# Down projections of a decoder layer: eight of 22 contraction slices as a block product with seven products instead of eight, per pair of output tiles

## The reference, cut to what matters

```python
D_MODEL, D_FF = 1024, 2816

def swiglu(x, w_gu, w_down):
    g, u = jnp.split(x @ w_gu, 2, axis=-1)
    return (jax.nn.silu(g) * u) @ w_down

def trunk_layer(x, ...):
    f1 = swiglu(rmsnorm(x, norm_ffn1_pre), w_ffn1_gu, w_ffn1_down)
    x = x + 0.5 * rmsnorm(f1, norm_ffn1_post)
    mix, state = mixer(rmsnorm(x, norm_mix_pre), ...)
    x = x + rmsnorm(mix, norm_mix_post)
    f2 = swiglu(rmsnorm(x, norm_ffn2_pre), w_ffn2_gu, w_ffn2_down)
    return x + 0.5 * rmsnorm(f2, norm_ffn2_post), state
```

## Time and profile before

| | |
|---|---|
| three runs | 1361.54, 1366.59, 1367.52 us; median 1366.59 |
| the profiled execution | 1366.81 us, its span 1364.8 us |
| PE busy | 1329.4 us (97%) |
| DVE, ACT busy | 874.6 (64%), 566.9 us (42%) |
| mean granted clock of TensorE | 0.986 of 2.4 GHz |
| first down stage | 253.5 to 385.9 us |
| last down stage | 1218.2 to 1350.6 us |

### The profile page before, as it was taken

One profiled execution on the slowest core, in us unless ns is written; L12 is line 12 of the kernel. 1 busy time (PEld: TensorE's weight loads), 2 busy tenths in 40 slices (PEclk: granted clock), 3 DMA queues, 4 the chain that ended last, 5 costly groups with the idle time before them and its releaser, 6 DMA issues. The chain is left out here.

```text
span 1364.8 us, 30387 instructions
## 1 busy us (share of the span) xinstructions
PE 1329.4 (97%) x11729; PEld 1247.5 (91%) x11729; DVE 874.6 (64%) x1689; ACT 566.9 (42%) x1064; POOL 145.1 (11%) x275
## 2 busy tenths in 40 slices
PE   8999999999999999999999999999899999999996
PEld 8999999999989978888789888869899999999995
DVE  5998899822277544554553566664899999983225
ACT  5455555722254334444352332233554555463221
POOL 0000000000003105555551000000000000000000
PEclk9999999999999999999999999979999999999998
DMA  4232233322245627777776133314252223332221
GB/s 161 92 124 93 94 105 125 129 86 85 93 158 189 214 85 218 240 212 219 204 224 246 48 124 142 125 48 157 80 189 94 93 96 119 123 112 98 87 83 66
DMA packets 81075, 180.20 MB, mean 132 GB/s; under 512 B 12137, under 2 KB 46954, under 8 KB 79146
## 3 DMA queue, kind: packets, MB, share of 16 engines
q1 hardware_dynamic: 72746, 161.56, 34.6%
q0 software_dynamic: 8192, 16.79, 4.3%
HBM read 162.01 MB, written 16.30 MB: 131 GB/s over the span
## 5 line engine op out<-in xcount | busy, mean ns | idle before, releaser
L921 PE MATMUL acc<-x_forms,pair_w 128*128 128x272 f32 x1728 | 273.1, 288 | 0.0
L921 PEld LDWEIGHTS acc<-x_forms,pair_w 128*128 128x128 f32 x1728 | 244.2, 188 | 0.0
L2029 DVE TENSOR_TENSOR w_lo<-w_raw,w_hi 128x1024 fp32r<-128x1024 f32 (+1 forms) x92 | 125.4, 1363 | 126.5 <-ACT w_hi L1435 126.5
L998 PE MATMUL acc<-x_hi,w_hi 128*128 128x272 f32 x656 | 199.5, 304 | 0.0
L998 PE MATMUL acc<-x_hi,w_lo 128*128 128x272 f32 x656 | 191.8, 292 | 0.0
L998 PE MATMUL acc<-x_lo,w_hi 128*128 128x272 f32 x656 | 191.6, 292 | 0.0
L1435 ACT ACTIVATE w_hi<-w_raw 128x1024 fp32r<-128x1024 f32 (+1 forms) x92 | 107.5, 1169 | 143.6 <-PE acc L740 79.7
L450 POOL DMA_DIRECT2D pg<-in_lat x256 | 138.3, 540 | 200.1 <-issue 134.7
L998 PEld LDWEIGHTS acc<-x_hi,w_hi 128*128 128x128 f32 x656 | 123.6, 188 | 9.5 <-issue 7.9
L998 PEld LDWEIGHTS acc<-x_lo,w_hi 128*128 128x128 f32 x656 | 123.7, 188 | 5.2 <-issue 4.7
L740 PE MATMUL acc<-h_hi,w_hi 128*128 128x272 f32 x616 | 127.2, 288 | 0.0
(11 more groups left out here) (394 smaller groups left out, 2535.4 us busy)
## 6 DMA issues: line engine op xcount, KB each, us to landing
w_pair<-in_w_gu SPq DMA_DIRECT2D x68, 512.0 KB, 4.2
pg<-in_key_t SPq DMA_DIRECT2D x256, 96.0 KB, 2.5
w_raw<-in_w_dn SPq DMA_DIRECT2D x32, 704.0 KB, 4.1
w_raw<-in_w_in SPq DMA_DIRECT2D x44, 512.0 KB, 4.4
pg<-in_lat POOLq DMA_DIRECT2D x256, 64.0 KB, 2.8
w_raw<-in_w_gu SPq DMA_DIRECT2D x20, 512.0 KB, 3.8
x_mid<-x SPq DMA_DIRECT2D x2, 2176.0 KB, 7.1
g_mid<-sq SPq DMA_DIRECT2D x16, 272.0 KB, 3.4
```

What stands on the lines that cost most here:

```text
L921: ins = nc.tensor.matmul(bank, w[:, k * P:(k + 1) * P], v[:, k, :], start=start and k == 0 and term == 0, stop=k == KD // 2 - 1 and term == 2,
L998: ins = nc.tensor.matmul(acc[0][:, a, 0:HT], w[:, i % 2, k * P:(k + 1) * P], v[:, k, a * HT:(a + 1) * HT], start=k == 0 and term == 0, sto ...
L2029: nc.vector.tensor_tensor(wlo[:, slot, 0:tiles * P], raw[:, slot, 0:tiles * P], f32(whi[:, slot, 0:tiles * P]), ALU.subtract).then_inc(w_s ...
```

## The change

KC = 14 slices of h stay direct: units have seven slices (896 columns), 42 matmuls. The other eight slices (7 to 10 and 18 to 21) form a 2 x 2 x 2 block product for each pair of output tiles: two tiles, two groups of four slices, two token halves. Seven products of four slices, three terms and one half (12 matmuls each) take the place of eight. For that ACT and DVE make, once per stage, four differences of h blocks and seven high and low parts of them (`form`, `form_hi`, `form_lo`, 4 x 272 = 1088 columns each), and once per pair four sums of weight blocks (`block_sums`) and seven splits (`block_hi_part`, `block_lo_part`, 512 columns each). The weight blocks lie in the ends of the unit slots and in freed buffers, so SP loads those of a pair when PE has used those of the pair before. The results are put together by two copies on ACT and seven additions on DVE (`take`, 272 columns). The last two tiles, not one, are summed by halves; the second half of tile 7's direct units comes last. x is loaded again in two parts.

The core of the diff, without the bookkeeping of counters, semaphores and the helpers that only name buffers:

```diff
 STAGE = {}
 _u = _g = 0
-for _name, _n, _t, _gr in (("gu1", NC, KD, NC), ("dn1", 2 * KD, 11, KD), ("in", 44, KD, 0),
-                           ("out", KD, KD, KD), ("gu2", NC, KD, NC), ("dn2", 2 * KD, 11, KD)):
+for _name, _n, _t, _gr in (("gu1", NC, KD, NC), ("dn1", 2 * KD, KC // 2, 1), ("in", 44, KD, 0),
+                           ("out", KD, KD, KD), ("gu2", NC, KD, NC), ("dn2", 2 * KD, KC // 2, 1)):
...
+        HALF_C = KC // 2
+        DIRECT = list(range(HALF_C)) + list(range(KF // 2, KF // 2 + HALF_C))
...
+        NORMAL, LAST = [A11, S1, S2, A12, S4, S3, A22], [A11, S1, S2, S4, S3, A22, A12]
+        HI_FIRST = [A11, A12, A22, S1, S2, S4, S3]
+        TAKE_NORMAL = ["part", "y11", "y12", "pg", "tq", "y22", "y21"]
+        TAKE_LAST = ["part", "y12", "pg", "y22", "tq", "y21", "y11"]
...
+            def down_stage(name, q):
+                for p in range(4):
+                    weight_units(name, 4 * p, 2)
+                    if p:
+                        sp.wait_ge(dn_used, 7 * (4 * q + p))
+                    else:
+                        sp.wait_ge(pair_split, 7 * (NP * (q + 1) - 1))
+                    for i, n in enumerate((A11, A12, S4, A22)):
+                        sp.dma_start(block_raw[n][:], weights[name][4 * p + i][:, HALF_C * P:]).then_inc(dn_raw, 16)
+                    if p == 0:
+                        sp.wait_ge(pair_used, 7 * NP * (q + 1))
+                        sp.dma_start(x[:, 0:KD // 2, :], (x_mid if q else xT)[:, 0:KD // 2, :]).then_inc(x_again, 16)
+                    weight_units(name, 4 * p + 2, 2)
+                sp.wait_ge(dn_used, used_of(q, 3, S2))
+                sp.dma_start(x[:, KD // 2:KD, :], (x_mid if q else xT)[:, KD // 2:KD, :]).then_inc(x_again2, 16)
...
-            def down(name, h_at):
-                u0, n, _, g0, _ = STAGE[name]
-                def body(i):
-                    for j in range(4):
-                        start = isinstance(i, int) and i == 0 and j < 2
-                        if isinstance(i, int) and i == n // 4 - 1 and j >= 2:
-                            if j == 2:
-                                U, G = 4 * i + u0 + 2, 2 * i + g0 + 1
-                                last_by_half("f1post" if name == "dn1" else "f2post",
-                                             [(U, G, 1, range(11), True, False), (U + 1, G, 1, range(11, KF), False, True)],
-                                             hhi, hlo)
-                            continue
-                        unit(4 * i + (u0 + j), j % 2, 2 * i + (g0 + j // 2), j // 2, hhi, hlo,
-                             range(11 * (j % 2), 11 * (j % 2) + 11), j % 2 == 0, j % 2 == 1,
-                             h_ready if start else None, h_at + 11 * (j % 2))
-                trips(pe, n // 4, body)
...
+                def direct(u, sides, start):
+                    pe.wait_ge(w_split, u0 + u + 1)
+                    for n in range(KC // 2):
+                        k = DIRECT[HALF_C * (u % 2) + n]
+                        if u < 2:
+                            pe.wait_ge(h_ready, KC * q + HALF_C * u + n + 1)
+                        for term, (w, v) in enumerate(((whi, hhi), (whi, hlo), (wlo, hhi))):
+                            for a in sides:
+                                ins = nc.tensor.matmul(acc[u // 2 % 2][:, a, 0:HT], w[:, u % 2, n * P:(n + 1) * P],
+                                                       v[:, k, HALF[a]], start=start and n == 0 and term == 0,
+                                                       stop=u % 2 == 1 and n == KC // 2 - 1 and term == 2,
+                                                       skip_group_check=True)
+                        if sides == (1,) and u % 2 == 0 and n == 3:
+                            sum_half(norm, 0)
+                    return ins
+                def product(p, n):
+                    pe.wait_ge(dn_split, split_of(q, p, n))
+                    if p == 0:
+                        pe.wait_ge(hf_split, 7 * q + NORMAL.index(n) + 1)
+                    if n == A11:
+                        if p:
+                            pe.wait_ge(dn_kept, 2 * (4 * q + p))
+                        else:
+                            pe.wait_ge(gate_done, 2 * NP * (q + 1))
+                            pe.wait_ge(part_taken, 5 * NP * (q + 1))
+                    elif n == S2:
+                        pe.wait_ge(dn_kept, 2 * (4 * q + p) + 1)
+                    elif p and n in (S1, S3):
+                        pe.wait_ge(dn_taken, taken_of(q, p - 1, "part" if n == S1 else "tq"))
+                    start = n in (A11, S1, S3) or (p == 3 and n == A22)
+                    v_hi, v_lo, _ = h_form(n)
+                    for k in range(KD // 2):
+                        for term, (w, v) in enumerate(((block_hi[n], v_hi), (block_hi[n], v_lo), (block_lo[n], v_hi))):
+                            ins = nc.tensor.matmul(bank_of[n], w[:, k * P:(k + 1) * P], v[:, k, :],
+                                                   start=start and k == 0 and term == 0,
+                                                   stop=k == KD // 2 - 1 and term == 2, skip_group_check=True)
+                    ins.then_inc(dn_used, 1)
+                for p in range(4):
+                    last = p == 3
+                    if p:
+                        pe.wait_ge(dn_taken, taken_of(q, p - 1, "y12"))
+                    for i in range(2):
+                        direct(4 * p + i, (0, 1), i == 0).then_inc(w_used, 1)
+                    if p:
+                        pe.wait_ge(dn_taken, taken_of(q, p - 1, "y21"))
+                    for i in range(2):
+                        ins = direct(4 * p + 2 + i, (0,) if last else (0, 1), i == 0)
+                        if not last:
+                            ins.then_inc(w_used, 1)
+                    for n in (LAST if last else NORMAL):
+                        product(p, n)
+                pe.wait_ge(dn_taken, taken_of(q, 3, "y21"))
+                direct(14, (1,), False).then_inc(w_used, 1)
+                pe.wait_ge(dn_taken, taken_of(q, 3, "y11"))
+                direct(15, (1,), False).then_inc(w_used, 1)
...
-                        hi_part(u0 + NC, 0, 11)
-                        for k in range(6):
+                        hi_part(u0 + NC, 0, KC // 2)
+                        for k in range(8):
                             split_h_hi(q, k)
                     silu(s, 0)
...
                 nc.scalar.preload_act_table_set(LOG_EXP)
-                for k in range(6, 11):
+                for k in range(8, 11):
                     split_h_hi(q, k)
-                hi_part(u0 + NC + 1, 1, 11)
-                for k in range(11, KF):
+                hi_part(u0 + NC + 1, 1, KC // 2)
+                for k in range(11, KC):
                     split_h_hi(q, k)
...
+                act.wait_ge(pair_used, 7 * NP * (q + 1))
+                form_hi(A11)
+                form_hi(S1)
+                unit_hi(2)
+                form_hi(S2)
+                form_hi(A12)
+                block_hi_part(0, A11)
+                unit_hi(3)
+                block_hi_part(0, A12)
+                block_hi_part(0, A22)
+                form_hi(S4)
+                block_hi_part(0, S1)
+                block_hi_part(0, S2)
+                form_hi(S3)
+                form_hi(A22)
+                block_hi_part(0, S4)
+                block_hi_part(0, S3)
+                for p in range(4):
+                    if p < 3:
+                        unit_hi(4 * p + 4)
+                    act.wait_ge(dn_used, used_of(q, p, A11))
+                    if p:
+                        act.wait_ge(dn_taken, taken_of(q, p - 1, "y21"))
+                    nc.scalar.activation(rpre[:, HALF[0]], acc[2][:, 0, 0:HT], ACT.Copy).then_inc(dn_kept, 1)
+                    if p < 3:
+                        unit_hi(4 * p + 5)
+                    act.wait_ge(dn_used, used_of(q, p, S2))
+                    nc.scalar.activation(rpre[:, HALF[1]], acc[2][:, 0, 0:HT], ACT.Copy).then_inc(dn_kept, 1)
+                    if p < 3:
+                        act.wait_ge(dn_taken, taken_of(q, p, "y12"))
+                        square(norm, 2 * p)
+                        act.wait_ge(dn_taken, taken_of(q, p, "y21"))
+                        square(norm, 2 * p + 1)
+                        unit_hi(4 * p + 6)
+                        for n in HI_FIRST[:5]:
+                            block_hi_part(p + 1, n)
+                        unit_hi(4 * p + 7)
+                        for n in HI_FIRST[5:]:
+                            block_hi_part(p + 1, n)
+                act.wait_ge(dn_taken, taken_of(q, 3, "y12"))
+                square_half(norm, KD - 2, 0)
+                act.wait_ge(dn_taken, taken_of(q, 3, "y22"))
...
+                def form(i):
+                    out, a, b = ((t1, b12, b11), (t3, b22, b12), (t2, b22, t1), (t4, b21, t2))[i]
+                    if i == 0:
+                        dve.wait_ge(h_full, KF * (q + 1))
```

(57 more changed lines are left out.)

177 lines of the change are left out of this document (130 added, 47 removed).

## The result

| | before | after |
|---|---|---|
| median of the runs | 1365.6 us (5 runs, 1361.54 to 1367.52) | 1379.44 us (5 runs, 1376.49 to 1379.8) |
| ratio | | 1.0101, interval 1.008 to 1.0122 |
| profiled execution, its span | 1366.81, 1364.8 us | 1376.49, 1374.8 us |

The change costs 13.8 us, 1.0%, and the interval of the ratio lies above 1: slower. The profiled execution after is the fastest of its five, so the two traces differ by only 10.0 us. The program also began earlier in it: the first down stage, dn1, starts at 251.13 us and not at 253.52. So I measure the two down stages from their own first matmul.

What follows compares the result with a forecast made beforehand. PE's matmuls were taken to bound the down stages, and DVE, started by the first half's root, the stretches behind them. The profiled 1366.8 us plus 3.3 (first transition) and 4.9 (end) gave 1375 us; range 1364 to 1382.

Steps and rivals of the forecast that it cites:

- PE's saving, 5.6 us a stage: Each down stage: 96 fewer matmuls save 12.0 us in all; products cost 0.8 more, so 5.6 us less PE work per stage.
- First pair, 0.9, 0.9, 1.9, 0.4, 1.1: PE's waits in us before units 1, 2, 3, at the last product and at y12 before pair 1; together 5.2.
- Last pair, 1.3: PE waits 1.3 us before unit 15 in each stage's last pair, since DVE splits it too late.
- rival 4: Loads land 2 us later, making unit 15 1.6 us later and unit 11 0.4, both stages: 1379 us; chance 0.13.
- Stage end 1.5 later, root 4.5 later: Each down stage: 7.1 us waiting against 5.6 saved ends PE 1.5 later; the sum's place adds 3.0 to the root.
- The w_in units split ahead lie under the last products: nothing: End of stage: splitting the next stage's first weight units ahead is hidden under the last products and costs 0 us.
- First transition, +3.3: After the first down stage, ACT squares the last half later; DVE goes on at 389.8 instead of 386.54: +3.3 us.
- The end, +4.9: After the last stage, DVE's row of 16 starts 4.5 us later; one more add costs 0.36: +4.9 us.
- No clock loss taken: PE keeps full speed after the new lone waits; no loss in the sum, 1.6 us a spell kept for the range.
- Rival 3: PE's clock falls at the waits: four spells of 1.6 us, 6.4 on top of the sum, 1381 us; chance 0.13.
- Rival 1: The waits do not come, ACT and DVE stay ahead in the first pair: 1361 us; chance 0.12.
- DVE's work in a steady pair: DVE's splits, sums, takes and square sums take 17 us per pair, within PE's 31.5 us.

Runs made afterwards that it cites:

- experiment 7: The changed kernel with the edits of experiment 1, experiment 2, experiment 5 and experiment 6 together: 1361.74 us.
- experiment 4: Against the changed kernel, DVE splits unit 15 of the last pair right behind the block sums, ahead of three block parts: 1375.02 us.
- experiment 6: experiment 4, and from the second pair on SP issues all four units of a pair ahead of its block weights: 1372.44 us.
- experiment 2: Against the changed kernel, SP issues the first two w_in loads after the last pair's product A11, ahead of x's second part: 1377.92 us.
- experiment 1: Against the changed kernel, the first half's sum is issued after the first of tile 7's last slices, not the fourth: 1377.27 us.
- experiment 3: Against the changed kernel, first-pair units 2 and 3 are split ahead of the differences' high parts on ACT, unit 3 before DVE's last difference: 1375.34 us.
- experiment 5: experiment 3, and in the first pair the take y12 stands ahead of unit 5's split on DVE: 1370.69 us.
- experiment 8: experiment 7, and behind the last stage DVE adds tile 6's second half after the fourth pair of the last row: 1360.13 us.

## Why the prediction was right, and where it was off

The direction and the mechanism were right: the forecast was 1375 against a median of 1379.4, with 8.2 us for the change against 13.8. The kind of each wait and its releaser came as written; most terms were sized too small. Part of the closeness is luck: the sum started from 1366.8, and the five runs before have a median of 1365.6.

- **PE's saving, 5.6 us a stage**: right. Experiment 7's stage takes 127.70, with gaps of 0.85 and 0.41 in it, which are 1.01 us above ordinary distances. Without them it is 126.7, against 132.3 before: 5.6 (5.8 without the 0.1 us of each restart).
- **First pair, 0.9, 0.9, 1.9, 0.4, 1.1**: measured 0.73, 0.89, 1.81, 0.30 and 1.10 (each gap less 0.125), 4.8 in place of 5.2. The hand-made schedule of DVE and ACT was good to 0.2 us. The restart is also as written: 257.08 to 257.44 is 0.36 instead of 0.25.
- **Last pair, 1.3**: it was 2.65 in dn1 and 1.78 in dn2. I took the loads' landing time from a kernel that had no blocks in the way (4 us). Unit 14, behind four blocks, landed 5.88 us after its issue in dn1 and 5.01 in dn2; ACT started unit 14 at 7.7 us behind the first block's issue, where my hand schedule had 6.4. Experiments 4 and 6 show both halves of the wait, DVE's order and SP's. Loads that land later were rival 4, which added 1.6 us to this wait and had a chance of 0.13; 1.35 more came in dn1 and 0.48 in dn2. Its 1379 us is the measured time, but by chance: it had 4 us from late loads at units 11 and 15, and the traces show 1.8.
- **Stage end 1.5 later, root 4.5 later**: in dn2 1.2 and 4.6. The 4.6 is partly luck: the sum came 4.2 later, and 0.4 stands between ACT's root and DVE's first step (1353.29 to 1353.77, before 1344.82 to 1344.93), which no term had and whose cause is open. In dn1 2.1 and 6.9.
- **"The w_in units split ahead lie under the last products: nothing"**: this is the step that failed. SP issues their loads behind x's second part, which I had at "nothing" in the sentence before. Root 3.41 behind the sum instead of 1.64 costs 1.8 us: 1.5 is the late load (experiment 2), and 0.3 the second unit's splitting, which doesn't lie under the products either. I costed the move of x's load by its own landing, not by what stands behind it on SP.
- **First transition, +3.3**: measured 7.0. DVE's add for the second half came 5.5 us later (138.55 against 133.02 from the stage's start), 2.2 more than forecast: 1.8 from w_in and 0.6 from a sum that was 5.1 late and not 4.5, less 0.2. Then PE's nine matmuls at half the clock ahead of the second sum took 0.95 more, where I had PE at full speed, and from that sum to the root it was 0.49 more (1.14 for 0.65). 5.5 + 0.95 + 0.5 is the 7.0.
- **The end, +4.9**: measured 5.75. The root gave 4.6. The row grew by 1.1 and not 0.36: the two adds are chained (the sum starts 1.06 us behind the first of them, where it started 0.49 behind the only one), and the sum behind them took 1.28 instead of 0.73, at a granted clock of 0.50 and not 1.00.
- **No clock loss taken**: half right. Behind the first pair's gaps (0.85 to 1.93 us) no trace shows a fall, and after's own gap of 2.77 cost nothing beyond its length either. But experiments 1, 2, 3 and 5 each had one fall behind a gap of 2.1 to 3.0 us, 1.6 us in three of them and 1.4 in experiment 3. Four of after's five runs lie 2 to 3.3 us above its profiled one. A fall that the profile didn't catch could do that, but the mean granted clocks don't settle it (0.991, 0.986, 0.986 and 0.988 there, 0.987 in the profiled run), and dn1's start alone lies anywhere from 250.73 to 255.59 us in the traces of after and the experiments; it stays open. Rival 3, "the clock falls at the waits", was thus right on the last gap in some executions and wrong on the others. The Trainium skill, "TensorE: Matmul & The Clock Gate", section "HAM oscillation — how this bites in real kernels", tells of a kernel that falls back at every wait; its waits were of some 3 to 5 us. I read it as a rule for all six gaps of a stage, which are shorter than that. The traces show no fall at the five short ones, and in four stages a fall behind the longest, at 2.14 to 3.02 us.
- **Rival 1 (no waits, 1361)**: experiment 7 comes near that case, with 1361.7, but the likeness of the two numbers is chance: rival 1 had 6.0 us less than before (3.8 + 2.2), and experiment 7 has 3.0, with the sum moved 1.1 us forward besides. Its first half's root is 1.3 us earlier in dn1 and 2.3 in dn2; 2.6 had been written, with every gap gone.
- **DVE's work in a steady pair**: the listed steps add up to 16.4 us, not 17; nothing rests on it. And the two rows named for full speed, 931.82 and 932.14, are 0.32 us apart, the restart included; the 0.25 a pair comes behind them.

What stays open: which gap makes the clock fall; and unit 1's 0.85, the same in all nine traces of the changed kernel. The prediction puts it down to eight h tiles being split ahead of the bank's take instead of six; going back to six wasn't tried in a run, so that isn't shown.

## What to carry to other kernels

A cut in TensorE's work is worth its matmuls only if the helpers deliver in the order in which TensorE asks. Write out each helper's queue and each load queue by hand against the time at which PE wants the item; a helper that is 70% busy overall still makes PE wait when one item stands three places too late, and swapping lines gets it back. When loads are added or split, price everything that is queued behind them too. And where a sum is followed by a chain over several engines, the time that the chain adds is read at its last consumer, not at the sum.

## What the runs showed of the hardware

- The clock after a gap in dense work isn't settled by the gap's length alone in these traces. 2.77 (after, dn1), 2.74 (experiment 5, dn1), 2.46 (experiment 1, dn1) and 1.90 (after, dn2) kept 1.00, and so did 2.91 behind dn1 in experiment 8; 2.54 (experiment 2), 2.63 (experiment 1, dn2), 2.14 (experiment 5, dn2) and 3.02 (experiment 3) fell to half. Behind three of these falls 16 matmuls took 0.227 us instead of 0.125; in experiment 3 it was 12.
- A lone pair of matmuls at the end of a chain of waits took 0.73 us at a granted clock of 1.00 (before, 1.80 us idle), 0.87 at 0.76 (experiment 7, 4.62 idle) and 1.27 and 1.28 at 0.50 (experiment 8, 4.27 idle; after, 5.75 idle). Its price went with the clock, not with the length of the idling.
- What is queued ahead of a load counts more than its size: 448 KB landed after 3.1 to 3.4 us when issued alone, and after 5.0 to 6.8 us right behind four loads of 256 KB; 704 KB had a median of 4.1.
